# Three modulation rows of layer 0 spread over the partitions by TensorE instead of through DRAM

## The chip, the cores and the metric

One core of a Trainium2 chip runs the whole program. The metric is device time in microseconds (us); a median of three runs is given for the kernel before. PE is TensorE (PEld its weight loads), DVE is VectorE, ACT is ScalarE, POOL is GpSimd, SP is SyncE, whose queue carries the weights.

## The reference, cut to what matters

Two blocks of two layers each are applied to x, 256 tokens by 1024 features, in float32. The change is in layer 0 of the first block:

```python
mod = c_act @ ada_w[l] + ada_b[l]
shift_m, scale_m, gate_m, shift_f, scale_f, gate_f = jnp.split(mod, 6, axis=-1)
h = rms_norm(x, g_pre_mix[l]) * (1.0 + scale_m) + shift_m
...   # projection, windowed attention, pooling
mix = jnp.concatenate([attn_out, pool_out], axis=-1) @ w_out[l]
x = x + gate_m * rms_norm(mix, g_post_mix[l])
h = rms_norm(x, g_pre_ffn[l]) * (1.0 + scale_f) + shift_f
f = (silu(h @ w_gate[l]) * (h @ w_up[l])) @ w_down[l]
x = x + gate_f * rms_norm(f, g_post_ffn[l])
```

The six parts of `mod` have 1024 elements each and are the same for all tokens. `gate_m`, `scale_f` and `shift_f` of layer 0 are the three rows of the change.

## The kernel before

Tokens lie on the partitions in two halves (T = 0, 1) in `x`, and are turned to features on partitions for the products. Each float32 product is done as three fp32r matmuls (L473 to L475) on a high and a low part of weights and data: ACT rounds the high part (`prepare`, L1041, and copies into `in_hi`), DVE subtracts it to get the low part (`lo`, L1380, and `in_lo`).

All weights come on SP's queue in the fixed order of `UNITS`, a unit of 1 MB (0.64 MB for `ink`) at a time. The loop at L914 has NRAW = 4 slots `raw_w`: the transfer of unit n is issued when unit n-4 has been used up, by `lo` or, for a modulation unit, by `ada`. Behind it are NSPLIT = 3 slots of `hi_w` and `lo_w`, which PE frees.

The modulation is not computed on PE. `ada(l, n)` lets DVE multiply a 1 MB unit of `ada_w` with the row of c and sum it up, two instructions at L1390, for 256 of the 6144 outputs. Every fourth unit completes a row, and `mod_column` (L1402 to L1408) adds bias and gain into `modcol`, where the row's 1024 numbers lie as 128 partitions by 8. Layer 0's units stand in this order around the change: wo2, a8, a9, a10, wo3, a11 (gate_m complete), a16, a17, wo0, a18, a19 (scale_f complete), a12, wo1, a13, a14, a15 (shift_f complete), gu0, gu1, gu2, a20, gu3 and so on. DVE takes them in the same order.

What uses such a row multiplies it along the free axis, for which it must stand on all 128 partitions, in `rows` (slot 0 gate, 1 scale, 2 shift). `mod_row` (L961 to L968) does that on POOL's queue: a DMA writes the 128 by 8 numbers of `modcol` to DRAM in row order, so that each of the 1024 numbers goes to a place of its own (L965), POOL waits for its end, and a second DMA reads the 4 KB row back to all partitions (L953). For layer 0 POOL's program reads: gate_m row, scale_f row, shift_f row, each with its waits; then `scale(("ffn", 0), 0, 0)`, which multiplies x with the scale row (L983).

At the end of a mixer, `ending` (L555) lets PE finish y = mix in four blocks: wo0 and wo1 for T = 0, wo0 and wo1 for T = 1; then `turn_norm` transposes the normalized h of T = 0, `front(0)` multiplies it with gu0 and gu1, and the same follows for T = 1. `chain` is the same stretch on ACT (L1058) and DVE (L1459): ACT takes squares of y (`root`, L1047 to L1056), DVE does `gained` = y * gate row (L1428) and x += gained * rstd (L1433), ACT takes squares of x, POOL does `scaled` = x * scale row, and DVE does `normed` = scaled * rstd + shift row (L1449). After this the feed-forward part of the layer runs on PE, its weights coming two gu units, one wd unit and two modulation units at a time.

At the start (`started`, L1083) the eight `ink` units are handled in four pairs j. ACT prepares unit 2j, rounds `in_hi` of tiles 2j and 2j+1 when DVE has scaled them, and then prepares unit 2j+1; for j = 1 it loads an activation table, waits for the angles from POOL (`turns`), takes their sine and loads the first table again before `in_hi`.

Of the kernel before, what the change touches and what calls it, by code (L numbers as in the profile page):

```python
# [14 lines left out]
P = 128  # L15
# [248 lines left out]
def build(nc, counts, a_x, a_pos, a_const, const_at, a_vec, a_w, a_bias, a_norm, a_cnorm, a_sinks, a_gatew, a_poolw, a_c, out):  # L264
    ctx = ExitStack()
    with ctx:
# [173 lines left out]
        def _(pe):  # L440
# [114 lines left out]
            def ending(L, w, one, other, front):  # L555


                N = after(L, w)
                into_y(L, w, one, 0)
                into_y(L, w, other, 0, last=True)  # L560
                into_y(L, w, one, 1)
# [32 lines left out]
            def attention_windowed(L):  # L594
# [329 lines left out]
        def _(pool):  # L924
# [11 lines left out]
            pool.wait_ge(*due("pos_in", 0))  # L936
            pool.wait_ge(*due("const_in", 0))
            step(nc.gpsimd.tensor_copy(pos_f, pos_i))
            for T in range(2):
                step(nc.gpsimd.tensor_scalar(ang[:, 8 * T:8 * T + 8], k("freq"), pos_f[:, T:T + 1], None, ALU.mult))  # L940
            for i, quarter in ((0, 0.25), (1, 0.0)):

                step(nc.gpsimd.tensor_scalar(whole, ang, 1.0 / two_pi, quarter, ALU.mult, ALU.add))
                step(nc.gpsimd.tensor_scalar(whole, whole, magic, None, ALU.add))
                step(nc.gpsimd.tensor_scalar(whole, whole, magic, None, ALU.subtract))
                for n, c in enumerate(parts):
                    step(nc.gpsimd.tensor_scalar(part, whole, c, None, ALU.mult))
                    step(nc.gpsimd.tensor_tensor(turns[:, i, :], ang if n == 0 else turns[:, i, :], part, ALU.subtract))
                step(nc.gpsimd.tensor_scalar(turns[:, i, :], turns[:, i, :], quarter * two_pi, -3.1415925, ALU.add, ALU.max))
                nc.gpsimd.tensor_scalar(turns[:, i, :], turns[:, i, :], 3.1415925, None, ALU.min).then_inc(*sig("turns", i))  # L950
# [4 lines left out]
            pool.wait_ge(*due("ada", ("ada", 0, 7)))  # L955
            load(bias, a_bias[0:1, :], 1280, "bias_in", 0)
            pool.dma_start(sinks[:, :, :], a_sinks.rearrange("(o l) n -> o l n", o=1).to_broadcast([P, 2, HEADS])).then_inc(*sig("sinks_in", 0, by=16))
            pool.dma_start(poolw[:, :, :, :], a_poolw.rearrange("l g c d -> c l g d")).then_inc(*sig("poolw_in", 0, by=16))
            pool.dma_start(gatew[:, :, :], a_gatew.rearrange("l g n -> g l n")).then_inc(*sig("gatew_in", 0, by=16))

            def mod_row(L, kind, w):  # L961
# [3 lines left out]
                pool.dma_start(mod_rows[n, :].rearrange("(t p) -> p t", p=P), modcol[:, n, :], allow_slow_non_contiguous=True).then_inc(*sig("row_out", n, by=16))  # L965
                pool.wait_ge(*due("row_out", n))
                slot = ("gate", "scale", "shift").index(kind)
                load(rows[:, slot, :], mod_rows[n:n + 1, :], D, f"row{slot}", L, kind, w)  # L968

# [4 lines left out]
            def scale(N, L, w):  # L974

                for T in range(2):
                    for c in range(2):
                        pool.wait_ge(*due("x", L, w, T, c))
                        if T == 0 and c == 0:
                            pool.wait_ge(*due("row1", N[1], "scale", 0 if N[0] == "mix" else 1))  # L980
# [5 lines left out]
            mod_row(0, "gate", 0)  # L986
            mod_row(0, "scale", 1)
            mod_row(0, "shift", 1)
# [12 lines left out]
            pool.wait_ge(*due("scaled", ("mix", 1), 1, 1))  # L1001
# [5 lines left out]
            pool.wait_ge(*due("scaled", ("ffn", 1), 1, 1))  # L1007
# [14 lines left out]
        def _(sc):  # L1022
# [47 lines left out]

# [12 lines left out]
            def started():  # L1083
# [9 lines left out]
                for j in range(4):  # L1093
                    prepare(("ink", 0, 2 * j))
                    if j == 1:
# [8 lines left out]
                    prepare(("ink", 0, 2 * j + 1))  # L1104

            def attention_windowed(L):
# [44 lines left out]
                for jp in range(2):  # L1151
                    sc.wait_ge(*due("attn", L, jp))
                    nc.scalar.activation(in_hi[:, 2 * jp:2 * jp + 2, :], ps(("attn", L, jp))[:, :], ACT.Identity).then_inc(*sig("attn_hi", L, jp))
                prepare(("gu", L, 0))
# [202 lines left out]
        def _(ve):  # L1357
# [56 lines left out]
            def residual(L, w, T):  # L1414
# [449 lines left out]
```

## Time and profile before

| | |
|---|---|
| median of 3 runs | 1273.38 us (1272.33 to 1275.3) |
| profiled execution, time | 1265.9 us |
| its span, first to last instruction | 1264.1 us |
| PE / DVE / ACT / POOL busy | 1145.6 / 842.0 / 644.2 / 53.8 us |
| mean granted TensorE clock | 0.970 |
| HBM read | 253.79 MB |

The profile gives busy time by engine, the chain of work that ended last, and groups of instructions by line. Waits are given as the engine and line that waited and what released it. Times inside the execution count from the span's start.

### The profile page before, as it was taken

What the parts mean: (1) busy time and instruction counts of PE and PEld (TensorE: products, weight loads), DVE (VectorE), ACT (ScalarE), POOL (GpSimd) and SP (SyncE); (2) the same over time, 40 slices, a digit from 0 to 9 for tenths busy, and PEclk for the clock granted to TensorE, in tenths of its full rate; (3) what the DMA queues carried; (4) which work ended last, traced back from release to release, by engine and by line L of the source; (5) the groups of instructions that cost most, each with busy time, mean ns of one, the idle gap of its engine ahead of it and who ended that gap; (6) DMA issues with size and microseconds to landing.
All of it is one profiled execution on the core that took longest, in us unless ns stands there. A gap on an engine that the chain in (4) does not pass through costs nothing.

```text
span 1264.1 us, 19698 instructions
## 1 busy us (share of the span) xinstructions
PE 1145.6 (91%) x7883; PEld 1041.7 (82%) x7883; DVE 842.0 (67%) x1324; ACT 644.2 (51%) x1126; POOL 53.8 (4%) x73
## 2 busy tenths in 40 slices
PE   2759299999985989999999999999999999999998
PEld 2547299999874789999988879999989878999996
DVE  4897587877786466555567666765667756765664
ACT  4433363434543564444475566655456566654553
POOL 3200100000010010000000000000000000000000
PEclk9978699999997999999999999999999999999999
DMA  7978669999759237668644234555553523465540
GB/s 288 327 279 214 204 256 303 356 258 373 289 143 257 85 134 276 209 231 235 219 142 180 101 134 161 208 193 192 180 190 128 194 92 136 157 217 192 178 164 34
DMA packets 38363, 256.16 MB, mean 203 GB/s; under 512 B 4704, under 2 KB 4992, under 8 KB 9984
## 3 DMA queue, kind: packets, MB, share of 16 engines
q1 hardware_dynamic: 34416, 242.50, 56.8%
q0 software_dynamic: 3136, 10.42, 2.4%
q10 hardware_dynamic: 720, 1.97, 0.4%
q8 instruction: 63, 1.03, 0.3%
q14 instruction: 28, 0.23, 0.0%
HBM read 253.79 MB, written 1.09 MB: 202 GB/s over the span
## 4 chain that ended last, share of the span: by engine, by line
PE 73%; DVE 11%; DMA 7%; ACT 4%; issue 3%; POOL 1%; ACTq 0%; DVEq 0%; POOLq 0%
PE bank L473 23%; PE bank L475 23%; PE bank L474 23%; DMA raw_w<-weights 5%; DVE lo_w L1380 3%; PE bank L480 2%; DVE raw_w L1390 2%; DMA start<-positions 1%; ACT gtok L1047 1%; DVE in_lo L1470 1%; DMA sinks<-sink_rows 1%; ACT hi_w L1041 1%; DVE prob L1490 1%; DVE smax L1493 1%; PE bank L520 1%
## 5 line engine op out<-in xcount | busy, mean ns | idle before, releaser
L1380 DVE TENSOR_TENSOR lo_w<-raw_w,hi_w 128x1024 fp32r<-128x1024 f32 (+4 forms) x370 | 433.0, 1192 | 155.0 <-ACT hi_w L1041 154.1
L1041 ACT ACTIVATE hi_w<-raw_w 128x1024 fp32r<-128x1024 f32 (+4 forms) x370 | 370.5, 1026 | 194.1 <-DMA raw_w<-weights 98.9
L473 PE MATMUL bank<-in_hi,lo_w 128*128 128x256 f32 x1408 | 395.7, 281 | 0.0
L474 PE MATMUL bank<-in_lo,hi_w 128*128 128x256 f32 x1408 | 393.0, 279 | 0.0
L475 PE MATMUL bank<-in_hi,hi_w 128*128 128x256 f32 x1408 | 392.9, 279 | 0.0
L473 PEld LDWEIGHTS bank<-in_hi,lo_w 128*128 128x128 f32 x1408 | 264.3, 188 | 2.5 <-issue 0.8
L474 PEld LDWEIGHTS bank<-in_lo,hi_w 128*128 128x128 f32 x1408 | 263.7, 187 | 1.9 <-issue 0.5
L475 PEld LDWEIGHTS bank<-in_hi,hi_w 128*128 128x128 f32 x1408 | 264.6, 188 | 0.0
L473 PE MATMUL bank<-hi_w,in_lo 128*128 128x256 f32 (+2 forms) x544 | 178.1, 327 | 29.8 <-DVE in_lo L1541 12.3
L474 PE MATMUL bank<-lo_w,in_hi 128*128 128x256 f32 (+2 forms) x544 | 174.6, 321 | 0.0
L475 PE MATMUL bank<-hi_w,in_hi 128*128 128x256 f32 (+2 forms) x544 | 174.4, 321 | 0.0
L473 PEld LDWEIGHTS bank<-hi_w,in_lo 128*128 128x128 f32 x544 | 106.7, 196 | 44.9 <-issue 19.7
L473 PE MATMUL bank<-hi_w,hid_lo 128*128 128x512 f32 x352 | 139.2, 396 | 0.5 <-DVE lo_w L1380 0.5
L474 PE MATMUL bank<-lo_w,hid_hi 128*128 128x512 f32 x352 | 139.0, 395 | 0.0
L475 PE MATMUL bank<-hi_w,hid_hi 128*128 128x512 f32 x352 | 139.0, 395 | 0.0
L1390 DVE SCALAR_TENSOR_TENSOR raw_w<-raw_w,c_row 128x1024 f32<-128x1024 f32 x96 | 113.2, 1218 | 18.2 <-DMA raw_w<-weights 9.6
L475 PEld LDWEIGHTS bank<-hi_w,in_hi 128*128 128x128 f32 x544 | 106.4, 196 | 7.6
L474 PEld LDWEIGHTS bank<-lo_w,in_hi 128*128 128x128 f32 x544 | 106.8, 196 | 6.9
L475 PEld LDWEIGHTS bank<-hi_w,hid_hi 128*128 128x128 f32 x352 | 66.1, 188 | 16.0
L473 PEld LDWEIGHTS bank<-hi_w,hid_lo 128*128 128x128 f32 x352 | 66.1, 188 | 14.9 <-DVE lo_w L1380 0.8
L474 PEld LDWEIGHTS bank<-lo_w,hid_hi 128*128 128x128 f32 x352 | 66.1, 188 | 14.3
L1301 ACT ACTIVATE shared<-bank,vcol 128x256 f32<-128x256 f32 x44 | 24.7, 562 | 98.8 <-PE bank L475 91.1
(200 smaller groups left out, 1011.9 us busy)
## 6 DMA issues: line engine op xcount, KB each, us to landing
raw_w<-weights SPq DMA_DIRECT2D x219, 1024.0 KB, 5.0
raw_w<-weights SPq DMA_DIRECT2D x8, 640.0 KB, 6.2
rows<-mod_rows POOLq DMA_DIRECT2D x10, 512.0 KB, 8.8
rows<-norm_rows POOLq DMA_DIRECT2D x5, 512.0 KB, 5.0
raw_w<-weights SPq DMA_DIRECT2D x2, 832.0 KB, 4.4
const<-const_table SPq DMA_DIRECT2D x1, 1538.0 KB, 8.1
raw_w<-weights SPq DMA_DIRECT2D x2, 768.0 KB, 4.6
shared<-bias_rows POOLq DMA_DIRECT2D x2, 640.0 KB, 10.4
```

What stands on the lines that cost most here:

```text
L473: nc.tensor.matmul(o, st[1], mv[0], start=start, stop=False, **kw)
L474: nc.tensor.matmul(o, st[0], mv[1], start=False, stop=False, **kw)
L475: return nc.tensor.matmul(o, st[0], mv[0], start=False, stop=stop, **kw)
L480: last = nc.tensor.matmul(o, w, r, start=(i == 0), stop=(i == len(pairs) - 1))
L520: last = nc.tensor.transpose(b[:, P * i:P * (i + 1)], s_, k("ident"))
L1041: nc.scalar.activation(hi_w[:, m % NSPLIT, cut], raw_view(unit)[:, cut], ACT.Identity).then_inc(*sig("hi_w", unit, i))
L1047: nc.scalar.activation(junk[:, :], src(c), ACT.Square, accum_out=ssq[:, T, c:c + 1]).then_inc(*sig("squared", *key, T, c))
L1301: nc.scalar.activation(conv[:, f % 2, :], ps(("gu", L, f))[:, 0:256], ACT.Identity, bias=v(f"conv_b{l}", f), scale=v(f"conv_w{l}", 44 + f) ...
L1380: nc.vector.tensor_tensor(lo_w[:, m % NSPLIT, cut], raw_view(unit)[:, cut], hi_w[:, m % NSPLIT, cut].bitcast(F32), ALU.subtract).then_inc( ...
L1390: last = nc.vector.scalar_tensor_tensor(w[:, f, :], w[:, f, :], 1.0, c_row[:, :], ALU.mult, ALU.mult, accum_out=mods[:, l, 2 * n + f:2 * n ...
L1470: nc.vector.tensor_tensor(in_lo[:, 4 * c:4 * c + 4, s_], by_tile(ps(("tr", N, T, c))[:, :]), in_hi[:, 4 * c:4 * c + 4, s_].bitcast(F32), A ...
L1490: nc.vector.scalar_tensor_tensor(pr[:, :, 0:w], ps(job)[:, 0:nh * w].rearrange("p (h k) -> p h k", h=nh), scale, bcast(mask, nh), ALU.mult ...
```

## The change

- `spread_row` on PE: for each of the eight tiles of a row, the column of `modcol` repeated 128 times is the stationary operand and the identity the moving one, a plain float32 matmul; its result has element p of the tile in column p on every partition. Eight matmuls of 128 columns fill two banks. The gate row's stand at the end of layer 0's attention, the scale row's between the blocks of y for T = 0 and T = 1, the shift row's behind the last block of y.
- `row_in` on ACT: two copies of 512 columns from PSUM into `rows`. The gate row's stand ahead of gu0's `prepare`, the scale row's between the two `root` of T = 0, the shift row's behind the first half of gu1's `prepare`.
- The consumers wait for these copies, half a row at a time.
- POOL no longer writes and reads back these three rows (six DMAs). Layer 1's bias load (640 KB) moves from behind layer 1's first two rows to the point where layer 0's evacuations are done, ahead of `scale(("ffn", 0), 0, 0)`. Layer 1's shift row is now written ahead of its scale row.
- At the start, ACT prepares unit 2j+1 of each pair directly behind unit 2j.
- `bank` use: `banks(4, 5, 6, 7)` is called before the scale row. The moved `lo` at n = 2 and the written-out ada(0, 13) to ada(0, 15) leave DVE's order as it was, as `angles` does POOL's.

```diff
@@ ending
                 into_y(L, w, other, 0, last=True)
+                if opening:
+                    banks(4, 5, 6, 7)
+                    spread_row(0, "scale", 1)
                 into_y(L, w, one, 1)
...
                     into_y(L, w, other, 1, last=True)
+                    if opening:
+                        spread_row(0, "shift", 1)
                     turn_norm(N, 0)
...
+            def spread_row(L, kind, w):
+
+                pe.wait_ge(*due("modcol", L, kind, w))
+                for c in range(2):
+                    job = ("spread", L, kind, w, c)
+                    b = take(job)
+                    for i in range(4):
+                        t = 4 * c + i
+                        last = nc.tensor.matmul(b[:, P * i:P * (i + 1)], modcol[:, ROWS[(L, kind, w)], t:t + 1].to_broadcast([P, P]), k("ident"),
+                                                start=True, stop=True)
+                    last.then_inc(*sig(*job))
@@ attention_windowed, PE
                     attention(q)
+                if L == 0:
+                    spread_row(0, "gate", 0)
@@ gpsimd
+            angles()
             pool.wait_ge(*due("ada", ("ada", 0, 7)))
...
+            pool.wait_ge(*due("tok", 0, 1, 2))
+            load(bias, a_bias[1:2, :], 1280, "bias_in", 1)
...
-            mod_row(0, "gate", 0)
-            mod_row(0, "scale", 1)
-            mod_row(0, "shift", 1)
             scale(("ffn", 0), 0, 0)
 
             pool.wait_ge(*due("normed", ("ffn", 0), 1, 1))
             mod_row(0, "gate", 1)
-            pool.wait_ge(*due("scaled", ("ffn", 0), 1, 1))
+            mod_row(1, "shift", 0)
             mod_row(1, "scale", 0)
-            mod_row(1, "shift", 0)
-            pool.wait_ge(*due("tok", 0, 1, 2))
-            load(bias, a_bias[1:2, :], 1280, "bias_in", 1)
             scale(("mix", 1), 0, 1)
@@ chain, ACT
                     root("rstd_post", (L, w), T, 0, lambda c: due("y", L, w, T, c), lambda c: ps(("y", L, w, T, c))[:, :])
+                if (L, w, T) == (0, 0, 0):
+                    row_in(0, "scale", 1)
                 root("rstd", (N,), T, 1, lambda c: due("x", L, w, T, c), lambda c: x[:, T, cols(c)])
...
                 prepare(following, (0,))
+                if (L, w, T) == (0, 0, 0):
+                    row_in(0, "shift", 1)
...
+            def row_in(L, kind, w):
+
+                slot = ("gate", "scale", "shift").index(kind)
+                for c in range(2):
+                    copy(("spread", L, kind, w, c), rows[:, slot, cols(c)], ps(("spread", L, kind, w, c))[:, :], "row", L, kind, w, c)
@@ started, ACT
                     prepare(("ink", 0, 2 * j))
+                    prepare(("ink", 0, 2 * j + 1))
...
-                    prepare(("ink", 0, 2 * j + 1))
@@ residual and norm, DVE
-                ve.wait_ge(*due("row0", L, "gate", w))
+                if (L, w) != (0, 0):
+                    ve.wait_ge(*due("row0", L, "gate", w))
                 for c in range(2):
+                    if (L, w) == (0, 0):
+                        ve.wait_ge(*due("row", 0, "gate", 0, c))
...
-                        ve.wait_ge(*due("row2", N[1], "shift", 0 if N[0] == "mix" else 1))
+                        if N == ("ffn", 0):
+                            ve.wait_ge(*due("row", 0, "shift", 1, c))
+                        else:
+                            ve.wait_ge(*due("row2", N[1], "shift", 0 if N[0] == "mix" else 1))
```

## Rows read from the trace of the kernel before

**Rows 1.** Waits, 95 to 175 us: us in total, times, longest us.
```profile
PE bank L520 <- DVE normed L1449: 21.6, 1, 21.6
```
**Rows 2.** Chain that ended last: start us, us, what.
```profile
107.16 4.59 DVE raw_w L1390 x8
...
114.45 14.61 DMA raw_w<-weights
...
131.96 0.90 POOL mod_rows L965
132.86 12.29 issue
...
151.00 0.76 DVE normed L1449
```
**Rows 3.** Windows: busy us (count) of PE, PEld, DVE, ACT, POOL; PEclk, DMA share, GB/s.
```profile
104.00:112.00 8.00, 8.00 (x48) 6.35 (x48) 7.14 (x12) 1.71 (x2) 0.00 (x0) 0.91 0.93 380
120.00:128.00 8.00, 8.00 (x36) 6.41 (x35) 4.35 (x8) 0.00 (x0) 0.56 (x1) 1.00 0.79 171
136.00:144.00 8.00, 0.00 (x0) 0.00 (x0) 2.35 (x4) 3.53 (x10) 0.00 (x0) 0.50 1.00 149
196.00:204.00 8.00, 8.00 (x51) 7.13 (x50) 4.63 (x8) 1.56 (x3) 0.00 (x0) 1.00 1.07 109
```
**Rows 4.** POOL's timeline: two of the writes, start us, us.
```profile
112.43 0.90 POOL L965 DMA_DIRECT2D mod_rows<-modcol  x1 [9.16 <-DVE modcol L1408]
...
192.03 0.94 POOL L965 DMA_DIRECT2D mod_rows<-modcol  x1 [30.51 <-DVE modcol L1407]
```
**Rows 5.** DMA issues: KB each, median us to landing; whole span, then 112 to 130 us.
```profile
raw_w<-weights SPq DMA_DIRECT2D x219, 1024.0 KB, 5.0
...
raw_w<-weights SPq DMA_DIRECT2D x5, 1024.0 KB, 14.4
```
**Rows 6.** DVE in order of time: start us, us busy.
```profile
119.51 0.76 DVE L1632 TENSOR_TENSOR in_lo<-bank,in_hi 128x256 fp32r<-128x256 f32 x2 [1.51 <-ACT in_hi L1153]
...
133.47 2.36 DVE L1380 TENSOR_TENSOR lo_w<-raw_w,hi_w 128x1024 fp32r<-128x1024 f32 x2 [1.81 <-ACT hi_w L1041]
135.75 1.28 DVE L1428 TENSOR_TENSOR gained<-bank,rows 128x512 f32<-128x512 f32 x2
136.95 1.40 DVE L1433 SCALAR_TENSOR_TENSOR x<-gained,tok_rstd,x 128x512 f32<-128x512 f32 x2
...
157.73 1.40 DVE L1433 SCALAR_TENSOR_TENSOR x<-gained,tok_rstd,x 128x512 f32<-128x512 f32 x2
160.81 1.92 DVE L1449 SCALAR_TENSOR_TENSOR normed<-scaled,tok_rstd,rows 128x512 f32<-128x512 f32 x2 [1.69 <-ACT tok_rstd L1056]
```
**Rows 7.** ACT in order of time, 135 to 141 us.
```profile
135.19 0.58 ACT L1047 ACTIVATE gtok<-bank 128x512 f32<-128x512 f32 x1
...
139.91 1.04 ACT L1041 ACTIVATE hi_w<-raw_w 128x1024 fp32r<-128x1024 f32 x1
```
**Rows 8.** PE in order of time: float32 matmuls and transposes.
```profile
94.01 3.75 PE L480 MATMUL bank<-pooled,poolw 128*128 128x256 f32 x8 [4.78 <-issue]
...
117.04 1.80 PE L480 MATMUL bank<-probT,tok 128*64 128x128 f32 x24
...
151.80 1.97 PE L520 MATMUL bank<-const,normed 128*128 128x128 f32 x8 [21.57 <-DVE normed L1449]
...
162.68 1.04 PE L520 MATMUL bank<-const,normed 128*128 128x128 f32 x8
```
**Rows 9.** ACT at the start, 32 to 39 us.
```profile
32.48 1.37 ACT L1041 ACTIVATE hi_w<-raw_w 128x640 fp32r<-128x640 f32 x2 [5.96 <-DMA raw_w<-weights]
33.86 1.28 ACT L1096 ACT_TABLE_LOAD   x1
...
37.43 0.72 ACT L1103 ACTIVATE in_hi<-raw 128x256 fp32r<-128x256 f32 x2
```
**Rows 10.** Waits of PE for weights, 160 to 340 us.
```profile
PE bank L473 <- DVE lo_w L1380: 0.5, 1, 0.5
```

More of the change, by code:

```diff
@@ L935, in _, with angles @@
             parts = (6.28125, 0.0019350051879882812, 3.019915982e-07)
[L936 to L950, printed above, removed]
+            def angles():
+                pool.wait_ge(*due("pos_in", 0))
+                pool.wait_ge(*due("const_in", 0))
+                step(nc.gpsimd.tensor_copy(pos_f, pos_i))
+                for T in range(2):
+                    step(nc.gpsimd.tensor_scalar(ang[:, 8 * T:8 * T + 8], k("freq"), pos_f[:, T:T + 1], None, ALU.mult))
+                for i, quarter in ((0, 0.25), (1, 0.0)):
+                    step(nc.gpsimd.tensor_scalar(whole, ang, 1.0 / two_pi, quarter, ALU.mult, ALU.add))
+                    step(nc.gpsimd.tensor_scalar(whole, whole, magic, None, ALU.add))
+                    step(nc.gpsimd.tensor_scalar(whole, whole, magic, None, ALU.subtract))
+                    for n, c in enumerate(parts):
+                        step(nc.gpsimd.tensor_scalar(part, whole, c, None, ALU.mult))
+                        step(nc.gpsimd.tensor_tensor(turns[:, i, :], ang if n == 0 else turns[:, i, :], part, ALU.subtract))
+                    step(nc.gpsimd.tensor_scalar(turns[:, i, :], turns[:, i, :], quarter * two_pi, -3.1415925, ALU.add, ALU.max))
+                    nc.gpsimd.tensor_scalar(turns[:, i, :], turns[:, i, :], 3.1415925, None, ALU.min).then_inc(*sig("turns", i))
@@ L952, in load @@
             def load(dst, src, n, name, *key):
                 pool.dma_start(dst, src.to_broadcast([P, n])).then_inc(*sig(name, *key, by=16))
[L955 to L958, printed above, removed]
@@ L968, in mod_row @@
                 load(rows[:, slot, :], mod_rows[n:n + 1, :], D, f"row{slot}", L, kind, w)
+            def mod_row(L, kind, w):
+                row_out(L, kind, w)
+                row_back(L, kind, w)
             def plain_row(N):
@@ L978, in scale @@
                         pool.wait_ge(*due("x", L, w, T, c))
-                        if T == 0 and c == 0:
-                            pool.wait_ge(*due("row1", N[1], "scale", 0 if N[0] == "mix" else 1))
+                        if T == 0:
+                            row = (N[1], "scale", 0 if N[0] == "mix" else 1)
+                            if row != (0, "scale", 1):
+                                pool.wait_ge(*due("row1", *row))
+                            else:
+                                pool.wait_ge(*due("row", *row, c))
                         if T == 1:
@@ L984, in scale @@
                             *sig("scaled", N, T, c))
-            mod_row(0, "gate", 0)
-            mod_row(0, "scale", 1)
-            mod_row(0, "shift", 1)
+            angles()
+            pool.wait_ge(*due("ada", ("ada", 0, 7)))
+            load(bias, a_bias[0:1, :], 1280, "bias_in", 0)
+            pool.dma_start(sinks[:, :, :], a_sinks.rearrange("(o l) n -> o l n", o=1).to_broadcast([P, 2, HEADS])).then_inc(*sig("sinks_in", 0, by=16))
+            pool.dma_start(poolw[:, :, :, :], a_poolw.rearrange("l g c d -> c l g d")).then_inc(*sig("poolw_in", 0, by=16))
+            pool.dma_start(gatew[:, :, :], a_gatew.rearrange("l g n -> g l n")).then_inc(*sig("gatew_in", 0, by=16))
+            pool.wait_ge(*due("tok", 0, 1, 2))
+            load(bias, a_bias[1:2, :], 1280, "bias_in", 1)
             scale(("ffn", 0), 0, 0)
@@ L1006, in _ @@
             mod_row(1, "gate", 1)
-            pool.wait_ge(*due("scaled", ("ffn", 1), 1, 1))
             plain_row(("mix", 2))
@@ L1153, in attention_windowed @@
                     nc.scalar.activation(in_hi[:, 2 * jp:2 * jp + 2, :], ps(("attn", L, jp))[:, :], ACT.Identity).then_inc(*sig("attn_hi", L, jp))
+                if L == 0:
+                    row_in(0, "gate", 0)
                 prepare(("gu", L, 0))
@@ L1607, in attention_windowed @@
                         evacuate(1, n - 1, 2)
+                    if n == 2:
+                        lo(("wo", 0, 3) if L == 0 else ("wo", 1, 0))
                     if L == 0 and n == 1:
                         ada(0, 10)
-                    if n == 2:
-                        lo(("wo", 0, 3) if L == 0 else ("wo", 1, 0))
                     if L == 0 and n in (3, 4, 5):
@@ L1633, in attention_windowed @@
                                                 ALU.subtract).then_inc(*sig("cat_lo", L, t, frees=("attn", L, jp)))
-                behind(("wo", L, 1))
+                if L == 0:
+                    for n in (13, 14, 15):
+                        ada(0, n)
                 lo(("gu", L, 0))
```

11 lines of the change are left out of this document (7 added, 4 removed).

## The prediction

> **What bounds the kernel now.** Read the waits first, then the chain, then the windows. From 130 us on PE stands still for 21.6 us, waiting for `normed` of layer 0 [rows 1]. The chain of waits shows what `normed` had to wait for [rows 2]: DVE has used up a12 at 114.4, then 14.6 us go to a weight transfer (a14, then a15), at 131.96 POOL issues the write of the shift row, 12.3 us later it is known to have ended, the row is read back, and DVE's `normed` starts at 151.00. From there PE is the chain: between 160 and 340 us its only wait for weights is one of 0.5 us [rows 10]. So whatever time `normed` gains, the end should gain.
>
> The windows show a second cost of the write [rows 3]. In a quiet stretch the weights come at 380 GB/s; in 120 to 128, 136 to 144 and 196 to 204 us, each 6 to 8 us behind such a write (POOL issued them at 112.4, 132.0 and 192.0, [rows 2, 4]), only 171, 149 and 109 GB/s move, while the DMA engines count as busy for 0.79 to 1.07 of the time. A row's 1024 numbers of 4 bytes hold up the 1 MB transfers beside them: a unit usually lands 5.0 us after its issue, those issued between 112 and 130 us after 14.4 us [rows 5]. The scale row's write of 112.4 us is thus what makes a14 and a15 late. The change takes away both the trip and the hold-up.
>
> **The change part by part.** All times are in the frame of before; `normed` at 151.00 is the mark.
>
> *Weights and DVE.* a13 is issued when a18 is used up, a14 and a15 at 111.7 and 114.4 (DVE uses two units in 4.59 us from 107.16, [rows 2]). At 5.0 us each, or one behind the other at 380 GB/s (2.8 us), a13, a14, a15 and gu0 land by 115, 118, 121 and 124 us. DVE cannot begin a13 before the last `in_lo` of the attention, at 119.51 + 0.76 - 0.1 = 120.2 [rows 6], as before. Three units at 2.3 us make 127.1, `modcol` 127.3, against 131.7 before: 4.4 us gained. Then gu0's `lo`, 2.36, to 129.7, `gained` and, 1.20 later, x from 130.9 [rows 6].
>
> *Spreading, PE.* No row shows a stationary operand that is one column repeated. Nearest are float32 matmuls with 128 moving columns: 12 calls (24 records) in 1.80 us at the full clock, 0.15 a call, so 1.2 us a row of 8; above, 4 calls of 256 columns in 3.75 us at half clock, so 3.75 us for 8 of 128 at half clock and 1.9 us at full [rows 8]. The clock of 120 to 128 us is 1.00 [rows 3]. I take 1.5, nearer to the first, which has its shape but for a narrower stationary side; ends 1.2 and 3.75. PE ran its four blocks of y from 118.8 (117.04 + 1.80) to 130.2 (151.80 - 21.57), 2.85 each [rows 8]. With the gate row ahead, y of T = 0 is there at 118.8 + 1.5 + 5.7 = 126.0; with the scale row, y of T = 1 at 133.2, and the shift row's first bank at 133.9, its second at 134.7.
>
> *Copies, ACT.* A copy of 512 columns from PSUM costs about 0.6 us (0.58 for the square of the same bank, [rows 7]). The gate row and gu0's high part are done by 125. The root of y follows, to 127.4, then the scale row's two copies to 128.6, ahead of x at 130.9: nothing waits for them. x to `normed` takes 160.81 - 157.73 = 3.1 us where no row is missing [rows 6]: 134.0. But the shift row's first copy lies behind it, after half of gu1's high part (1.04, [rows 7]): 134.0 + 1.05 + 0.6 = 135.7. So `normed` starts at 135.7 instead of 151.0: 15.3 us. Had the copy stood ahead, 1.7 more would be gained; late next is this copy, with PE's shift row one us before it.
>
> *PE's clock.* PE had stood for 21.6 us and was granted 0.50 [rows 3]; its 8 transposes took 1.97 us against 1.04 later [rows 8]. After the change it stands some 1 to 2 us. The first four are on the way; at the later rate they take some 0.4 us less, of which I take 0.3; the matmuls behind them are beside T = 1's chain, so at most 2.5 more.
>
> *Weights in the feed-forward part.* The slots are as full as before when it starts (gu1, gu2 and a20 are issued as DVE ends a13, a14 and a15, gu3 as it ends gu0's `lo` at 129.7, and all can land by 135). Four rows of layer 1 and the second gate row of layer 0 keep their trip, but they run beside a PE that is busy 8.00 of 8.00 us even at 109 GB/s [rows 3]. Layer 1's shift and scale rows are now apart, and the bias load no longer adds to them; the wait of 0.5 us [rows 10] should go. The bias load at 72 us costs nothing: 0.64 MB where the DMA engines have room; if that cover were gone, 1.7 us.
>
> *Start.* In pair 1 ACT now waits for the second `ink` unit before it loads the table. It lands one transfer of 0.64 MB (1.7 us at 380 GB/s) behind the first, at 34.2; the high part (1.37), the table twice (1.28 each) and the short sine between bring `in_hi` to about 38.4 instead of 37.43 [rows 9]. DVE then needs no wait of 0.5 us for the high part: 0.6 us lost, between 0 and 1.3. In the other pairs nothing changes: DVE has work without a gap. This loss runs on to the mark, since DVE and the bias load behind it shift along.
>
> *Moved lines without effect:* `lo` at n = 2 against ada(0, 10) at n = 1, the written-out loop, `angles`.
>
> Sum: -15.3 - 0.3 - 0.5 + 0.6 = -15.5 us. The profiled execution's own 1265.9 becomes 1250.4. The median of the runs lies 7.5 us above that execution; I take the same difference off it: 1273.4 - 15.5 = 1257.9.
>
> A DMA's fixed cost is about 2 us by the Trainium skill, DMA: Bandwidth & Descriptors, Latency and other measured facts. By that, write and read-back would be some 4 us together, and the sum would be about 11 us smaller, an estimate from that page. The trace has 12.3 us between issue and end of one such write [rows 2], and the trace decides (rival 6).
>
> **The rivals.**
> 1. The slow stretches are not the writes' doing. Then a14 and a15 stay late, `modcol` stays at 131.7, x at 136.95, and only the trip goes: `normed` at 136.95 + 3.1 + 1.7 = 141.7, gain 9.3 - 0.3 = 9, 1264. For it: the SP queue is limited by slots, which alone spaces transfers. Against: each of the three slow stretches stands behind a write.
> 2. PE's spreading is at the upper end, half clock or a slow load of the repeated column: with 3.75 a row, the shift row ends at 130.2 + 11.25 = 141.4, `normed` at 142: gain 9, again 1264.
> 3. More: the warm clock gives up to 2.5 us and the start costs nothing: 1254.5.
> 4. Nothing to be measured: the feed-forward part, begun 15 us earlier, uses up its lead at the writes of 192 and 222 us and gives the time back. For it: in 196 to 204 us the weights come at 109 GB/s. Against: with more disturbance (two writes and a bias load within 30 us) PE waited 0.5 us.
> 5. Slower: a zero-step stationary operand is read far slower than a plain one. All three rows lie ahead of T = 0's `normed`: it decides from 3 x G = 151.0 - 130.2 - 0.6 = 20 us, G = 6.7 us a row or 0.84 a matmul, against 0.15 to 0.47 in the rows. At 1.2 us a matmul the kernel would be slower by 8.6 us: 1282.
>
> 6. The trip is short in itself and `normed` waited behind something that stays. Then only the 4.4 us by which DVE is done earlier are gained: 1269.0. Against: `normed` starts 6 us behind the read-back's issue, and nothing else ends near it.
>
> **How the numbers follow.** Forecast 1257.9 (with 1256 to 1261): 0.62. Rivals 1 and 2: 0.14 and 0.06. Rival 3: 0.10. Rival 4: 0.03. Rival 5: 0.03. Rival 6: 0.02. The range takes in 3 and most of 1 and 2: 1254 to 1265. About 0.2% is what a measurement of this kernel can tell from no change: faster 0.94, same 0.03, slower 0.03.
>
> **What would show it.** Windows from 96 to 150 us near 380 GB/s whenever transfers are out, and units landing after about 5 us. `modcol` of the shift row near 127.9 (with the start's 0.6). `normed` near 136.3, and ACT's copy of the shift row just ahead of it. Spread matmuls of 1.2 to 1.9 us a row at clock 1.00. `in_hi` of pair 1 at 38.4. PE without a wait for `lo_w` between 145 and 325 us, and everything later shifted by one constant. Wrong would be: a gap of DVE before a14 or a15 (rival 1), PE's spreading beyond 2 us a row, PE waiting for weights in the feed-forward part, or a stretch after 340 us that differs in length from before.

## The result, and the profile after

| us | before | after |
|---|---|---|
| median of four runs each | 1272.86 (1271.61 to 1275.3) | 1253.28 (1250.32 to 1255.54) |
| profiled execution | 1265.9 | 1255.54 |
| its span | 1264.1 | 1253.6 |

After to before is 0.985, 95% interval 0.983 to 0.987: 19.6 us less where 15.5 were forecast. In microseconds the median lies 0.7 below 1254, the lower end of the forecast range; as a ratio it lies at the edge of that range (0.985 to 0.993 of 1273.4). The two profiled executions lie only 10.4 us apart, so the first thing to settle is which of these numbers belongs to the change. Their spans, cut at marks that both have (DVE's first evacuation of `tok`, then the first `normed` of each part), with a second profile of the kernel before (experiment 1):

| stretch, us | before | before again | after |
|---|---|---|---|
| start to first `tok` | 62.8 | 65.8 | 65.5 |
| to `normed` of layer 0's feed-forward part | 88.2 | 90.7 | 72.9 |
| to `normed` of layer 1's mixer | 194.7 | 199.1 | 195.2 |
| to `normed` of layer 1's feed-forward part | 97.6 | 98.5 | 98.6 |
| to the end | 820.9 | 821.4 | 821.4 |

Only the second row is clearly shorter against both profiles of before: 15.3 us against the first, 17.9 against the second. (The third is 3.9 us shorter than in the second profile, but 0.5 longer than in the first.) PE's waits in the changed kernel, 110 to 345 us (us in total, times, longest), which answer to [rows 1] and [rows 10]:
```profile
PE bank L520 <- DVE normed L1495: 3.9, 5, 1.5
PE bank L473 <- DVE in_lo L1516: 3.5, 3, 1.2
PE bank L473 <- DVE lo_w L1420: 1.5, 1, 1.5
```
The 21.6 us of standing are gone; no wait for `normed` is longer than 1.5. The chain of the changed kernel, 112 to 140 us (start us, us, what), answers to [rows 2]:
```profile
112.52 1.73 PE bank L480 x24
...
120.04 1.73 PE bank L480 x24
121.77 1.98 PE bank L589 x16
...
129.35 1.79 PE bank L589 x16
...
136.74 1.80 PE bank L589 x16
138.56 0.61 ACT rows L1114
139.26 0.76 DVE normed L1495
```
Neither a weight transfer nor POOL stands in it. PE has become the chain, and the three spreads (L589) stand in it with 1.8 to 2.0 us each. The windows (busy us and count of PE, PEld, DVE, ACT, POOL; PEclk, DMA share, GB/s) answer to [rows 3]:
```profile
120.00:128.00 8.00, 8.00 (x60) 7.00 (x60) 5.69 (x12) 3.68 (x5) 0.00 (x0) 1.00 0.76 285
136.00:144.00 8.00, 5.94 (x46) 5.17 (x45) 5.49 (x7) 6.44 (x16) 1.45 (x2) 1.00 0.16 65
196.00:204.00 8.00, 8.00 (x68) 7.86 (x67) 6.29 (x10) 4.98 (x7) 0.00 (x0) 1.00 1.01 419
256.00:264.00 8.00, 8.00 (x55) 7.27 (x54) 0.00 (x0) 0.90 (x1) 0.56 (x1) 1.00 0.68 100
```
Read the DMA share beside the rate: in 136 to 144 us little moves because little is asked for (share 0.16, the slots are full). In 256 to 264 us the share is 0.68 and only 100 GB/s move, and DVE does nothing at all for 8 us: that is the hold-up of [rows 3], now behind a write that the change has left in place (POOL issued it at 248.0 us). DVE and ACT around the mark (start us, us, idle before it and its releaser), against [rows 6]:
```profile
130.10 0.17 DVE L1442 TENSOR_TENSOR modcol<-mods,vcol 128x8 f32<-128x8 f32 x1
...
133.65 1.41 DVE L1476 SCALAR_TENSOR_TENSOR x<-gained,tok_rstd,x 128x512 f32<-128x512 f32 x2
138.40 1.61 DVE L1495 SCALAR_TENSOR_TENSOR normed<-scaled,tok_rstd,rows 128x512 f32<-128x512 f32 x2 [3.34 <-ACT rows L1114]
...
136.62 1.04 ACT L1069 ACTIVATE hi_w<-raw_w 128x1024 fp32r<-128x1024 f32 x1
137.67 0.60 ACT L1114 ACTIVATE rows<-bank 128x512 f32<-128x512 f32 x1
138.56 0.60 ACT L1114 ACTIVATE rows<-bank 128x512 f32<-128x512 f32 x1 [0.30 <-PE bank L589]
```

### The profile page after: what moved, and what is told of

Its sections match the earlier page's. It is cut to its first block, busy times and chain, and to the rows that moved or that the text cites. A ratio compares the mean times of both kernels' runs of the same rounds, so it can differ in the third digit from the quotient of the medians.

```text
span 1253.6 us, 19799 instructions
## 1 busy us (share of the span) xinstructions
PE 1150.2 (92%) x7931; PEld 1045.6 (83%) x7931; DVE 841.3 (67%) x1324; ACT 648.2 (52%) x1132; POOL 49.9 (4%) x67
## 3 DMA queue, kind: packets, MB, share of 16 engines
q10 hardware_dynamic: 720, 1.97, 0.4%
## 4 chain that ended last, share of the span: by engine, by line
PE 73%; DVE 12%; DMA 8%; ACT 4%; issue 2%; ACTq 0%; DVEq 0%; POOL 0%
PE bank L473 23%; PE bank L475 23%; PE bank L474 22%; DMA raw_w<-weights 6%; DVE lo_w L1420 3%; PE bank L480 3%; DVE raw_w L1430 2%; ACT gtok L1075 1%; DMA start<-vectors 1%; ACT hi_w L1069 1%; DMA sinks<-sink_rows 1%; PE bank L520 1%; DVE in_lo L1516 1%; DVE prob L1536 1%; DVE smax L1539 1%
## 5 line engine op out<-in xcount | busy, mean ns | idle before, releaser
L473 PEld LDWEIGHTS bank<-hi_w,in_lo 128*128 128x128 f32 x544 | 106.1, 195 | 44.8 <-issue 21.6
```

The lines of the kernel that those rows point to most:

```text
L473: nc.tensor.matmul(o, st[1], mv[0], start=start, stop=False, **kw)
```

## The experiments

Experiments 1 to 4 ran on one chip (there the kernel before took 1270.63 us), 5 to 8 on a second (1263.71), 9 to 12 on a third (1263.76). Ratios are to the kernel before on the same chip, with 95% intervals. The diffs are against the kernel after, for 1 and 5 against the one before.

**1. The kernel before again.** No edit.

> The kernel before, unchanged. The timed runs put the change at 19.6 us (1272.9 to 1253.3), the two profiled executions only at 10.4 (1265.9 to 1255.5). Theory A: the profiled execution of before was a short one by chance, and another has a span near 1271 us; the extra 7 us then lie in stretches where weight transfers are late (start, 0 to 63 us, or 95 to 151 us, or layer 1's attention, 360 to 400 us), not in one that PE bounds. Theory B: the profiled executions are typical and the timed ones carry 7 us outside the span: then the span is 1264 again.

1270.53 us (1267.38 to 1277.27), ratio 1.000 (0.998 to 1.002); the profiled execution took 1277.27. Its chain, against [rows 2]:
```profile
117.44 15.72 DMA raw_w<-weights
...
136.06 0.90 POOL mod_rows L965
136.96 13.57 issue
...
156.47 0.76 DVE normed L1449
```
The same three links, each somewhat longer, and the start 3.0 us longer too. So the profile on which the prediction rests was of a short execution, short at the start (62.8, where all thirteen later profiles, of any of these kernels, have 63.7 to 65.8) and in the feed-forward stretch (194.7 against 199.1 here).

**2. The rows written as before, but read by nobody.** POOL issues the three writes of layer 0 again, each when its row is complete; the consumers use TensorE's rows.
```diff
             pool.wait_ge(*due("tok", 0, 1, 2))
             load(bias, a_bias[1:2, :], 1280, "bias_in", 1)
+            row_out(0, "gate", 0)
+            row_out(0, "scale", 1)
+            row_out(0, "shift", 1)
             scale(("ffn", 0), 0, 0)
```


> The changed kernel, with POOL still writing the three rows of layer 0 to DRAM, which nobody reads. Theory (the writes hold up the weights): the scale row's write at 115 us leaves 120 to 128 us at about 170 GB/s, DVE waits some 4 us before a14 or a15, and normed of T = 0 comes 4 to 5 us later than 138.4; with the shift row's write behind it, 4 to 7 us longer in all, 1257 to 1260. Rival 1 (the late weights have another cause): no difference, 1253.

1257.87 us (1256.79 to 1260.84), ratio 0.990 (0.987 to 0.993). From `tok` to `normed` 78.6 us, where the kernel after has 72.9. DVE's row in order of time, the window, and the one wait of PE that is new, 110 to 345 us:
```profile
130.29 1.22 DVE L1433 SCALAR_TENSOR_TENSOR raw_w<-raw_w,c_row 128x1024 f32<-128x1024 f32 x1 [6.57 <-DMA raw_w<-weights]
```
```profile
120.00:128.00 8.00, 8.00 (x46) 6.92 (x47) 3.72 (x9) 1.76 (x3) 0.00 (x0) 1.00 1.08 92
```
```profile
PE bank L589 <- ACT rows L1117: 4.4, 1, 4.4
```
A write that nobody reads is enough to bring back the late unit: issued at 114.9 us, it leaves 92 GB/s in 120 to 128 us with the engines counted as busy. Set beside the kernel before on the same chip, this run also measures the trip by itself, since the writes are the same and only what the consumers read has changed (beside the edits that 4 and 8 undo): 90.7 us (experiment 1) become 78.6, and the median of 1270.6 us becomes 1257.9.

**3. The same bytes at the same times, in 128 pieces of 32 bytes.** The order in DRAM is another, which matters to nobody here.
```diff
+            def row_piece(L, kind, w):
+                n = ROWS[(L, kind, w)]
+                pool.wait_ge(*due("modcol", L, kind, w))
+                pool.dma_start(mod_rows[n, :].rearrange("(p t) -> p t", p=P), modcol[:, n, :]).then_inc(*sig("row_out", n, by=16))
+
+            row_piece(0, "gate", 0)
...
```


> As e2_writes_kept, but each partition's eight numbers go out as one piece of 32 bytes: 128 pieces instead of 1024, the same 4 KB, and nobody reads them. If the number of pieces makes the hold-up, an eighth of it stays: under 1 us against the changed kernel, 1253 to 1254. If any write to DRAM beside the weights does it, this costs as much as e2, 1257 to 1260.

1251.15 us (1249.9 to 1258.7), ratio 0.986 (0.982 to 0.989); `tok` to `normed` 72.7 us. The window:
```profile
120.00:128.00 8.00, 8.00 (x48) 6.74 (x45) 6.91 (x13) 4.47 (x8) 0.00 (x0) 1.00 0.79 290
```
290 GB/s, as in the kernel after (285), and DVE goes from a13 to a15 without a gap. 2 and 3 differ by the form of the write alone (number and size of the pieces, and their order in DRAM, which were not varied apart), and by 6.7 us of the median. In the profiles `normed` comes 5.9 us earlier after `tok`, and the stretch behind it is 2.1 us shorter (193.3 against 195.4). In 2 PE is granted only 0.59 and 0.56 in 136 to 152 us, behind its wait of 4.4 us; in 3 it is granted 0.82 and 0.97. The first rival is out: the slow stretches are the writes' doing, and what does it is a write in 1024 pieces of 4 bytes.

The Trainium skill, DMA: Bandwidth & Descriptors, Specifications, puts the least piece for full rate at 512 bytes and says that below it the engines read, modify and write. That puts 4 and 32 bytes on the same side; here the two differ by 6.7 us, and the measurement decides.

**4. The start undone.** ACT prepares unit 2j+1 where it did before.
```diff
                     prepare(("ink", 0, 2 * j))
-                    prepare(("ink", 0, 2 * j + 1))
...
                         nc.scalar.activation(in_hi[:, t, :], raw[:, t, :], ACT.Identity).then_inc(*sig("in_hi", N, t))
+                    prepare(("ink", 0, 2 * j + 1))
```


> The changed kernel with the start's order of before: ACT prepares unit 2j+1 behind in_hi of the pair. In the profile of the changed kernel in_hi of pair 1 came at 38.27 instead of 37.43 us, and the first evacuation at 65.5 instead of 62.8. Theory: 0.4 us of that are this edit, the rest is weights that happened to land later: 1252.9, a ratio of 0.9997. Rival: all 2.7 us are the edit: 1250.6.

1252.48 us (1251.85 to 1253.72), ratio 0.985 (0.982 to 0.989), the first `tok` at 65.0 us. DVE begins the first modulation unit behind pair 1 at 41.01 us here and at 40.94 in the kernel after: the edit at the start costs nothing that can be seen. Of the 2.7 us by which the first `tok` came later in the first profile of after, this leaves the edit 0.5 at most.

**5. The kernel before with 32-byte pieces for all ten rows.** The row in DRAM is then in the order (p, t), and the three consumers read `rows` with a stride of 8 elements.
```diff
-                pool.dma_start(mod_rows[n, :].rearrange("(t p) -> p t", p=P), modcol[:, n, :], allow_slow_non_contiguous=True).then_inc(*sig("row_out", n, by=16))
+                pool.dma_start(mod_rows[n, :].rearrange("(p t) -> p t", p=P), modcol[:, n, :]).then_inc(*sig("row_out", n, by=16))
...
+        def row_by_tile(slot, c):
+            return rows[:, slot, :].rearrange("q (s t) -> q t s", t=8)[:, 4 * c:4 * c + 4, :]
...
-                    nc.vector.tensor_tensor(gained[:, cols(c)], ps(job)[:, :], rows[:, 0, cols(c)], ALU.mult).then_inc(*sig("gained", *job))
+                    nc.vector.tensor_tensor(tiles(gained[:, cols(c)]), tiles(ps(job)[:, :]), row_by_tile(0, c), ALU.mult).then_inc(*sig("gained", *job))
```


> The kernel before, with all ten modulation rows still going by way of DRAM, but written as 128 pieces of 32 bytes; the row then lies tile-innermost and its three users read it with a stride of 8 numbers. It separates the hold-up from the trip. Theory (e2 and e3: the 1024 pieces are the cost): no slow windows, modcol of the shift row at 130.3 as in the changed kernel, then a short write (about 3 us) and the read-back (6 us), normed at 140 to 141; layer 1's attention gains some 8 to 10 us more by the same means. Some 1245, faster than the changed kernel. Rival (the trip through DRAM itself is the cost, whatever its pieces): normed stays at 150 or later, 1265 to 1268.

1263.43 us (1260.58 to 1266.34), ratio 1.000 (0.999 to 1.001). POOL's waits for the ends of its writes, first here, then in the kernel before:
```profile
POOL rows L959 <- DMA mod_rows<-modcol: 44.7, 10, 5.6
```
```profile
POOL rows L953 <- DMA mod_rows<-modcol: 119.7, 10, 14.5
```
A write ends after 4.5 us instead of 12, `tok` to `normed` is 75.7 us instead of 88.2 or 90.7, layer 1's attention 92.4 instead of 98. `normed` comes at 139.56 us, as the theory had it, but the 1245 us that it expected did not come: the time is that of before. T = 1 in this kernel, against [rows 6], where `normed` takes 1.92:
```profile
145.69 2.12 DVE L1434 TENSOR_TENSOR gained<-bank,rows 128x512 f32<-128x512 f32 x2
...
150.83 3.33 DVE L1455 SCALAR_TENSOR_TENSOR normed<-scaled,tok_rstd,rows 128x512 f32<-128x512 f32 x2 [1.69 <-ACT tok_rstd L1062]
```
The two feed-forward stretches take 199.6 and 200.9 us, where the kernel before had 194.7 and 195.0 (and 199.1 and 195.0 in its second profile; from this chip there is none). A large change, no effect on the time: in the profiles the gain is given back in the stretches in which the row is used. That the stride is the reason is read from the rows and was not tested by a run of its own; experiment 6 shows how it comes about.

**6. The kernel after with the same pieces for the seven rows that still go through DRAM.** The edit is that of 5, save for the reads of the three rows that TensorE spreads.

> The changed kernel, with the seven rows that still go by way of DRAM written as 128 pieces of 32 bytes. Theory: the weights' waits in layer 1's attention (DVE stands twice for them, 11 and 17 us on the chain) shrink to the transfers' own rate, 8 to 10 us gained; 1242 to 1245. Rival: layer 1's attention is bound by the rate of the weights, not by the writes: 1252.

1251.54 us (1248.67 to 1253.71), ratio 0.991 (0.989 to 0.992). Layer 1's attention falls to 90.6 us, and the next stretch, 193.8 in the kernel after, becomes 200.4. Against the 1250.86 that the kernel after took on a chip with the same time for before (9), nothing is left of the 8 to 10 us that were expected. The rival's number came (1252), but not its reason, since the attention did get shorter. In the stretch that grows by 6.6 us PE's waits for `normed` are 5.7 us in all instead of 1.7, and behind them PE is granted 0.57 of its clock where the kernel after keeps 1.00. The windows behind layer 1's attention, first here, then in the kernel after:
```profile
436.00:444.00 8.00, 6.83 (x34) 6.62 (x35) 3.41 (x4) 4.26 (x6) 0.00 (x0) 0.57 0.37 131
```
```profile
448.00:456.00 8.00, 8.00 (x71) 8.00 (x70) 4.72 (x4) 4.50 (x5) 0.00 (x0) 1.00 0.69 241
```
So the slower reads cost twice: 4.0 us as waits, and most of the rest, as the windows suggest, as matmuls at the lower clock (34 in 8 us instead of 71).

**7. Each spread done twice.** Twice the matmuls, the same result.
```diff
-                    for i in range(4):
+                    for i in (0, 1, 2, 3) * 2:
```


> The changed kernel, each spreading matmul done twice (same result). In its profile the chain from 112 to 138.6 us is PE: two attention products, y, and three spreads of 1.95 us. Theory: all three lie on the path, so 3 x 1.8 = 5.4 us more; 1258 to 1259. Rival (DVE or ACT sets normed, as the forecast had it): 1 us or less until PE is late, then 3 to 4 us, 1256.

1255.0 us (1253.95 to 1259.57), ratio 0.994 (0.992 to 0.996). PE's spreads in the chain, then the two halves of `normed` in DVE's order of time:
```profile
120.27 3.77 PE bank L589 x32
...
129.63 3.57 PE bank L589 x32
```
```profile
141.36 0.75 DVE L1495 SCALAR_TENSOR_TENSOR normed<-scaled,tok_rstd,rows 128x512 f32<-128x512 f32 x1 [7.81 <-ACT rows L1114]
143.12 0.75 DVE L1495 SCALAR_TENSOR_TENSOR normed<-scaled,tok_rstd,rows 128x512 f32<-128x512 f32 x1 [1.00 <-ACT rows L1114]
```
`tok` to `normed` is 77.2 us, 4.3 longer than in the kernel after. Each row takes 1.8 us more; the last row's second half is not needed for the first half of `normed`, so 5.4 - 0.9 = 4.5 us were added ahead of it, and 4.3 arrived. PE's time to spread is on the path. The kernel after itself did not run on this chip, so the medians do not test the expected 1258 to 1259.

**8. POOL's order for layer 1 as before.** Scale row before shift row, the bias load behind both.
```diff
-            pool.wait_ge(*due("tok", 0, 1, 2))
-            load(bias, a_bias[1:2, :], 1280, "bias_in", 1)
             scale(("ffn", 0), 0, 0)
...
             mod_row(0, "gate", 1)
-            mod_row(1, "shift", 0)
             mod_row(1, "scale", 0)
+            mod_row(1, "shift", 0)
+            pool.wait_ge(*due("tok", 0, 1, 2))
+            load(bias, a_bias[1:2, :], 1280, "bias_in", 1)
```


> The changed kernel with POOL's order for layer 1 as before: scale row ahead of shift row, back to back, and the bias load behind them instead of at 72 us. In the second profile of before, PE waited 4.4 us for weights and in_lo behind these two writes; in the changed kernel 1.5. Theory: this order costs 2 to 4 us in the feed-forward part of layer 0, 1255 to 1257. Rival (the lead of the weights covers it): no difference, 1253.

1248.49 us (1247.56 to 1250.18), ratio 0.989 (0.987 to 0.990). PE waits for no weights between 110 and 345 us, and from `normed` to layer 1's `normed` are 193.3 us, among the shortest of all the profiles (192.9 to 199.6). The 2 to 4 us that the theory expected the old order to cost are not there, and no gain of the new order can be seen; whether the 2.4 us under the 1250.86 of experiment 9 are more than the difference between two chips, these runs do not tell.

**9. The kernel after again,** as the reference for 10 to 12. No edit.

> The changed kernel once more, unaltered, beside the kernel before and the three variants below on one chip. By the theory (the change gains what it gains in the stage from the first evacuation of `tok` to `normed` of the feed-forward part, and the rest is shifted) the ratio to before is again near 0.985, and the profiled execution has about 72.9 us from the first `tok` to the first `normed`, 195 us from there to the next layer's `normed`, and 98.5 us through layer 1's attention. The rival (the gain depends on which chip it runs on, since on the second chip the kernel before was 7 us shorter) would give a ratio near 0.99.

1250.86 us (1248.95 to 1253.34), ratio 0.990 (0.988 to 0.991), `tok` to `normed` 72.8 us. Here the change brings 12.9 us and not 19.6. The kernel after is nearly the same on both chips (1253.3, 1250.9), the kernel before is not (1272.9, 1263.8): the rival that the expectation named has happened. The variants fit in: where the kernel before takes 1270.6 us, 3 and 4 are 19.5 and 18.2 us shorter, and where it takes 1263.7, 6 and 8 are 12.2 and 15.2 us shorter. Where before is shorter on this chip no profile shows.

**10. The gate row first, the shift row's copy first.** Two lines are moved.
```diff
                 banks(4, 5, 6, 7)
+                if L == 0:
+                    spread_row(0, "gate", 0)
                 for q, u in enumerate((2, 3)):
...
-                if L == 0:
-                    spread_row(0, "gate", 0)
@@ chain, ACT
-                prepare(following, (0,))
                 if (L, w, T) == (0, 0, 0):
                     row_in(0, "shift", 1)
...
+                prepare(following, (0,))
```


> The changed kernel with two moves. TensorE puts the gate row out before its first two blocks of y instead of behind them, where it waits for the attention's columns anyway; ScalarE takes the first two copies of the shift row before it prepares gu1's high part. By the theory that TensorE is the chain from 112 us on and each row costs it 1.95 us, the gate row's time disappears into a wait of TensorE and `normed` starts up to 1.9 us earlier, at least 1; the time falls by 1 to 2 us against the unaltered change. By the rival (TensorE has no idle time there, or DVE's modulation sum of the shift row is the later one) `normed` stays where it is and the time is the same within 0.5 us.

1248.58 us (1248.0 to 1249.54), ratio 0.988 (0.987 to 0.989), but `tok` to `normed` 72.5 us against 72.8: the expected 1 us is not there. A row of PE's order of time and one of the chain say why:
```profile
102.32 3.50 PE L589 MATMUL bank<-const,modcol 128*128 128x128 f32 x16 [0.22 <-DVE raw L1664]
```
```profile
122.24 6.88 DVE raw_w L1430 x12
```
In PE's idle time the granted clock is 0.57 (102 to 106 us), and the row costs 3.50 us instead of 1.95; the attention's columns come 0.8 us later behind it (counted from `tok`), DVE begins a13 later by as much, and now DVE's three units are the chain. The median is 2.3 us lower all the same. Of the 3.6 us between the two profiled spans 2.9 stand in the feed-forward stretch, 192.9 us here and 195.8 in 9, where PE was granted half clock for 4 us (last section); whether that is the edit's doing these runs do not show. The expectation's mechanism has failed here, whatever the median says.

**11. Layer 1's gate and second scale row written early.** POOL writes them behind layer 1's first two rows, where PE still has feed-forward work, and only reads them back where they were written and read before.
```diff
             mod_row(1, "scale", 0)
+            row_out(1, "gate", 0)
+            row_out(1, "scale", 1)
             scale(("mix", 1), 0, 1)
             pool.wait_ge(*due("normed", ("mix", 1), 1, 1))
-            mod_row(1, "gate", 0)
-            mod_row(1, "scale", 1)
+            pool.wait_ge(*due("row_out", ROWS[(1, "scale", 1)]))
+            load(rows[:, 0, :], mod_rows[ROWS[(1, "gate", 0)]:ROWS[(1, "gate", 0)] + 1, :], D, "row0", 1, "gate", 0)
+            load(rows[:, 1, :], mod_rows[ROWS[(1, "scale", 1)]:ROWS[(1, "scale", 1)] + 1, :], D, "row1", 1, "scale", 1)
```


> The changed kernel with the writes of layer 1's gate row and second scale row issued before GpSimd scales x for layer 1, and only read back where they are now written and read. The writes' 1024 pieces of 4 bytes then pass beside the feed-forward part's end and not beside layer 1's attention. The pieced variants showed the attention stage of layer 1 at 90.6 us instead of 98.5. By the theory that it is the writes that hold up that stage, it becomes 91 to 94 us here too, and since the layout in `rows` is unaltered nothing is given back: 5 to 7 us less than the unaltered change. By the rival (the writes cost their time wherever they stand) the feed-forward stretch before it, 195 us, grows by as much and the time is the same. A third way: the stage is shortened by what the pieces do to something else, then it stays at 98.5 us.

1239.8 us (1238.56 to 1245.0), ratio 0.982 (0.980 to 0.984), 11.1 us under the kernel after. Layer 1's attention takes 86.2 us instead of 96.0, and that is 9.8 of the 11.5 us between the two profiled spans. The stretch before it takes 193.9 us, no more than the 195.8 of 9. The chain of the kernel after on this chip (9), 344 to 380 us:
```profile
346.83 1.23 DVE lo_w L1420
...
348.07 11.09 DMA raw_w<-weights
...
359.18 1.07 ACT hi_w L1069
...
360.27 2.37 DVE lo_w L1420 x2
...
362.66 15.92 DMA raw_w<-weights
```
27 us of it are weight transfers behind two writes (POOL issued them at 344.8 and 354.6 us). In 11 the same stretch has none, and the two writes, now at 281.7 and 315.9 us, slow the weights where PE has work in stock:
```profile
288.00:296.00 8.00, 8.00 (x49) 7.00 (x48) 3.02 (x6) 2.32 (x3) 0.00 (x0) 1.00 0.76 152
```
152 GB/s, DVE busy for 3.02 of 8 us, PE for all 8. The place of a slow write decides what it costs.

**12. Experiments 10, 11 and 4 together.**

> The changed kernel with both moves above and with the order of pair 1 at the start as it was before the change. If the effects add, it lies 6 to 9 us under the unaltered change; if the early writes only shift their cost, 1 to 2 us under it.

1236.68 us (1235.2 to 1239.72), ratio 0.979 (0.977 to 0.980): 27.1 us under before and 14.2 under the kernel after, the fastest version here. More than the 6 to 9 us that were expected, since 11 alone brought more.

## Why the prediction was right, and where not

In the frame of before (2.73 us, by which the first `tok` is later, taken off) the steps up to the mark are these:

| | predicted | measured |
|---|---|---|
| `modcol` of the shift row | 127.3 | 127.4 |
| x | 130.9 | 130.9 |
| `normed` | 135.7 | 135.7 |
| gain of the stretch | 15.3 | 88.2 - 72.9 = 15.3 |

**The row trip and the hold-up** were both right in mechanism, and right in size for the execution from which they were read: 10.9 and 4.4 us. Other executions pay more. Experiments 1, 2 and 3, on one chip, show the two apart: the trip 12.1 us of the stretch and 12.8 of the median, the hold-up 5.9 and 6.7 (in the second profile of before DVE waits 5.1 us for the two units). Together that is 19.5 us of the median on that chip, as much as the 19.6 of the result, where the sum had 15.3 for both. With that the first rival is out, and the sixth. The units issued between 112 and 130 us land after 5.7 us (median) instead of 14.4 [rows 5].

**What is late next.** The copy of the shift row behind gu1's high part was named, and it is there: 136.62 + 1.04, then the copy at 137.67, then `normed`. PE's shift row was to be one microsecond before it. It is not: **G, the price of a row, was taken as 1.5 us and measures 1.95** (eight matmuls, 16 records each, from 121.70, 129.19 and 136.58 us; in the chain 1.8 to 2.0). In the frame of before its second bank was to be full at 134.7 us and was at 135.8. PE is now as late as the copy, and the second copy waits 0.30 us for it. The step that failed is the choice of the nearest row: of [rows 8], 24 records in 1.80 us have this shape but a narrower stationary side, and the other row taken at full clock gave 1.9 us, which was right. The forecast of `normed` survived by luck: the term was off the path by as much as it was wrong. Experiment 7 shows that the next microsecond is not free, and experiment 10 that at a granted clock of 0.57 the row costs 3.50 us, near the upper end of 3.75.

**A zero-step stationary operand** costs 0.24 us a matmul, against the 0.84 from which the fifth rival decided, and the 0.47 (3.75 a row) of the second.

**PE's clock.** It stays at 1.00 in 136 to 144 us, and four transposes take 0.66 us; from T = 0 to T = 1 `normed` takes 9.4 us instead of 9.8. The first four transposes are 0.32 us shorter than half of the 1.97 of [rows 8], as forecast (0.3). The third rival's further 2.5 us did not come: the sum had this stretch 0.8 us shorter than in the first profile of before, and it is 0.5 longer, with 1.0 us more of waiting for `lo_w` in it. (By its own terms that rival gives 1254.8 and not 1254.5; the measured median lies below both, for another reason, the size of trip and hold-up.)

**Weights in the feed-forward part** (-0.5): wrong. PE waited 1.5 us for `lo_w`, behind the write of 248.0 us, and not 0. The fourth rival had this place, though not its size: the lead is used up there in some executions (1.5 us in the first profile of after; none in 8, 9 and 10) and in before too (3.2 us in experiment 1). The prediction also passed over where the rows that keep their trip stand. There are seven and not five; three of them run beside the busy PE of which it speaks. Two more stand at the start of layer 1's attention, where a write costs most (experiment 11). That changed nothing in the forecast, since before pays for them too. And the slow windows of [rows 3] begin 4.0 to 7.6 us behind their writes, not 6 to 8.

**The start** (+0.6): nothing, by experiment 4. `in_hi` of pair 1 came at 38.3 us as summed up (38.4), but with the edit undone it comes at 37.8 and not at the 37.43 of [rows 9]; the 0.45 us that are left are just what DVE gains, which no longer waits 0.44 us for the high part. Half of what I put down to the edit was chance of one execution.

**The difference between the profiled execution and the median** is the step that was most wrong in size. I carried the 7.5 us by which the first profile of before lay under its median over to after. The profiled execution of after lies 2.3 us above its own. So the forecast for the profiled execution, 1250.4, was 5.1 us too low, that for the median 4.6 too high. Against the second profile of before, the stretch itself is shortened by 17.9 us, since the transfers behind a write and the trip vary from one execution to the next (14.6 and 15.7, 12.3 and 13.6 us), and a kernel that has lost them has lost their variation too. What this does not explain is the chip: 19.6 us of gain on one, 12.9 on another, and the forecast of 15.5 lies between by luck. That stays open. So does the sign that the prediction set itself, a stretch after 340 us that differs in length: 98.6 and 821.4 us are 1.0 and 0.5 longer than in the first profile of before and the same as in the second.

## What to carry to other kernels

When a wait ends at a small transfer, ask what that transfer does to the large ones beside it, and test the two apart: a write nobody reads, and the same bytes in larger pieces, took two runs. A slow write that can't be removed is moved to where the engine that sets the end has work in stock; on the chip of experiments 9 to 12 that was worth nearly as much as the change itself (11.1 us and 12.9), and nothing had to be computed in another way. And a forecast made against one profiled execution needs a second one before its distance from the median is carried over.

## What the runs showed of the hardware that I had not expected

- 4 KB to DRAM as 1024 pieces of 4 bytes end after 8 to 16 us (12.0 on average in the kernel before) and bring the 1 MB transfers beside them from some 290 to 420 GB/s down to 92 to 171 for a window of 8 us. As 128 pieces of 32 bytes they end after 4.5 us on average (5.6 at most), and no cost to the others can be seen: 290 GB/s in the window in question (experiments 2, 3, 5).
- DVE pays for a stride of 8 elements in one float32 operand: T = 1's two halves of `normed` take 3.33 instead of 1.92 us, of `gained` 2.12 instead of 1.28 (experiment 5).
- Waits of 1.5 and 1.2 us (1.49 and 1.17) leave the clock alone in one execution and halve it in another. In the profiles of experiments 4 and 8 PE has these two waits at the same place and is granted 1.00. The kernel after in experiment 9, windows of 4 us (columns as above):
```profile
148.00:152.00 4.00, 2.82 (x16) 2.38 (x15) 4.00 (x6) 3.42 (x4) 0.00 (x0) 0.65 0.00 0
152.00:156.00 4.00, 4.00 (x21) 4.00 (x21) 2.24 (x4) 0.75 (x2) 0.00 (x0) 0.50 0.72 266
156.00:160.00 4.00, 4.00 (x36) 4.00 (x36) 3.06 (x3) 3.15 (x4) 0.00 (x0) 1.00 0.64 264
```
  21 matmuls in 4 us instead of 36. In the first profile of after the same kernel had 1.00 in these windows, with waits of 1.3 and 1.2 us before them. The feed-forward stretch took 195.8 us here and 192.9 to 194.2 in experiments 3, 4, 8 and 10 to 12, in whose profiles it has full clock from 152 us on. The place counts and not the half clock alone: 3, 10 and 12 are granted 0.57 to 0.63 in 140 to 144 us, while T = 1's chain runs, and are the shortest or nearly so. The first profile of after has 195.2 us at full clock, 1.5 of them the wait for `lo_w`. That the clock is the whole of this difference was not tested by a run of its own.
